# Moving each granule's low product behind the next granule's high products, with a compact delta rule and a later wait for x

## The reference

```python
# gated_delta_rule, chunk length c = 64, 4 chunks, 8 heads (cut)
lower = where(strict, einsum('bhncd,bhnsd->bhncs', kb, k) * decay, 0.0)
tinv = triangular_solve(eye + lower, eye, lower=True, unit_diagonal=True)
u = tinv @ vb
w = tinv @ (kb * exp(g)[..., None])
qk = einsum('bhncd,bhnsd->bhncs', q, k) * decay
def step(state, inp):                      # lax.scan over the 4 chunks
    v_new = un - wn @ state
    o = (qn * exp(gn)[..., None]) @ state + qkn @ v_new
    state = state * exp(g_last) + einsum('bhck,bhcv->bhkv', kn * exp(g_last - gn), v_new)
    return state, o

# hybrid_layer (cut)
x = x + (g_a * (o_a @ w_pa) + g_b * (o_b @ w_pb)) @ w_o
h = rms_norm(x, ln2_w)
return x + square(relu(h @ w_up)) @ w_down
```

## Time and profile before

| what | value |
|---|---|
| median of 3 runs | 2716.54 us (2715.74 to 2717.14) |
| the profiled execution's own time | 2715.65 us |
| its span, first to last instruction | 2714.0 us |
| mean granted clock of TensorE | 0.997 |
| PE busy | 2689.3 us, 99% of the span |
| DVE busy | 1859.4 us, 69% |
| ACT busy | 1288.8 us, 47% |
| POOL busy | 87.3 us, 3% |
| moved by DMA | 504.90 MB, mean 186 GB/s |

### The profile page before, as it was taken

How to read it: one execution, slowest core, us unless ns; L and a number is a source line. 1 busy time by engine, 2 the same in 40 slices (tenths; PEclk the granted TensorE clock), 3 DMA queues, 4 the chain that set the end, 5 groups by cost and what they waited for, 6 DMA issues and landing times.

```text
span 2714.0 us, 35008 instructions
## 1 busy us (share of the span) xinstructions
PE 2689.3 (99%) x12765; PEld 2227.3 (82%) x12765; DVE 1859.4 (69%) x2453; ACT 1288.8 (47%) x1613; POOL 87.3 (3%) x106
## 2 busy tenths in 40 slices
PE   9999999999999999999999999999999999999998
PEld 7888887888888888888888888888888888888886
DVE  5565767765678668586678666775585966668766
ACT  6564646544455444344445555455354434434342
POOL 1000110100000000000000000000000000000000
PEclk9999999999999999999999999999999999999999
DMA  8765555556677666666666566675565656666663
GB/s 243 249 188 142 157 148 145 160 173 188 228 194 198 195 193 193 193 192 195 192 193 192 188 164 183 190 179 200 180 200 166 197 173 190 198 179 190 179 212 122
DMA packets 261739, 504.90 MB, mean 186 GB/s; under 512 B 16456, under 2 KB 25720, under 8 KB 260560
## 3 DMA queue, kind: packets, MB, share of 16 engines
q1 hardware_dynamic: 256848, 486.76, 59.8%
q0 software_dynamic: 4704, 16.03, 2.6%
q10 hardware_dynamic: 32, 0.01, 0.0%
HBM read 498.66 MB, written 4.08 MB: 185 GB/s over the span
## 4 chain that ended last, share of the span: by engine, by line
PE 97%; ACT 1%; DVE 1%; DMA 0%; issue 0%; SPq 0%; DVEq 0%; ACTq 0%
PE acc L296 53%; PE acc L303 27%; PE acc L1965 2%; PE acc L1963 2%; PE acc L1962 2%; PE acc L1923 1%; PE acc L1924 1%; PE acc L1922 1%; PE acc L2080 1%; PE acc L2089 1%; PE mx L511 1%; DMA res<-in_x 0%; PE mx L1741 0%; ACT w_hi L264 0%; PE mx L519 0%; PE mx L343 0%
## 5 line engine op out<-in xcount | busy, mean ns | idle before, releaser
L272 DVE TENSOR_TENSOR w_lo<-raw,w_hi 128x1024 fp32r<-128x1024 f32 x916 | 1121.1, 1226 | 738.0 <-ACT w_hi L264 720.4
L264 ACT ACTIVATE w_hi<-raw 128x1024 fp32r<-128x1024 f32 x916 | 967.7, 1059 | 1234.1 <-PE acc L303 1077.8
L296 PE MATMUL acc<-w_hi,lt_b_hi 128*128 128x512 f32 x1760 | 685.0, 389 | 0.0
L296 PE MATMUL acc<-w_hi,lt_b_lo 128*128 128x512 f32 x1760 | 684.8, 389 | 0.0
L296 PE MATMUL acc<-w_hi,lt_a_hi 128*128 128x512 f32 x1440 | 564.0, 392 | 0.7 <-DVE lt_b_lo L390 0.7
L296 PE MATMUL acc<-w_hi,lt_a_lo 128*128 128x512 f32 x1440 | 562.6, 391 | 0.0
L303 PE MATMUL acc<-w_lo,lt_b_hi 128*128 128x512 f32 x1760 | 476.8, 393 | 0.0
L303 PE MATMUL acc<-w_lo,lt_a_hi 128*128 128x512 f32 x1440 | 394.6, 396 | 1.2 <-DVE w_lo L272 1.2
L296 PEld LDWEIGHTS acc<-w_hi,lt_b_hi 128*128 128x128 f32 x1760 | 330.3, 188 | 68.8
L296 PEld LDWEIGHTS acc<-w_hi,lt_b_lo 128*128 128x128 f32 x1760 | 330.3, 188 | 68.8
L303 PEld LDWEIGHTS acc<-w_lo,lt_b_hi 128*128 128x128 f32 x1760 | 328.7, 188 | 70.3 <-issue 3.8
(11 more groups left out here) (415 smaller groups left out, 1835.1 us busy)
## 6 DMA issues: line engine op xcount, KB each, us to landing
raw<-in_ret_w_in SPq DMA_DIRECT2D x192, 512.0 KB, 4.0
raw<-in_w_in SPq DMA_DIRECT2D x168, 512.0 KB, 3.6
raw<-in_w_up SPq DMA_DIRECT2D x128, 512.0 KB, 3.8
raw<-in_w_down SPq DMA_DIRECT2D x128, 512.0 KB, 4.5
raw<-in_fox_w_in SPq DMA_DIRECT2D x128, 512.0 KB, 4.4
raw<-in_ret_w_out SPq DMA_DIRECT2D x64, 512.0 KB, 4.6
raw<-in_w_o SPq DMA_DIRECT2D x32, 512.0 KB, 4.5
raw<-in_fox_w_out SPq DMA_DIRECT2D x32, 512.0 KB, 4.6
```

The source lines that it names most:

```text
L264: nc.scalar.activation(w_hi[:, r % 4], raw[:, slot, 2 * half:2 * half + 2, :], ACT.Copy).then_inc(hi_ready, 1)
L272: nc.vector.tensor_tensor(w_lo[:, r % 4], raw[:, slot, 2 * half:2 * half + 2, :], w_hi[:, r % 4].bitcast(F32), ALU.subtract) \
L296: nc.tensor.matmul(acc[par][t][:, :], lt[p][:, kt, t * P:(t + 1) * P], w_hi[:, r % 4, k, :], start=(kt == 0 and p == 0), stop=False)
```

## The change

It has three parts.

First, `multiply` is written in another order. The low products become a function `low(r)`. In granule r PE now makes the high products of r, takes the step of the mix, and then makes the low products of granule r-1; the first granule has none, and the job ends with the low products of granule 7. `split_hi`, `split_lo`, `split_job` and their waits stay as they are. In the lines of the new kernel the low products are line 293 and the high ones line 307.

Second, the delta rule's chunk matrices become 64 columns wide: both chunks' blocks stand in the same columns, one above the other on the partitions. `by_chunk` goes; its two operations of 64 x 512 become one of 128 x 512, and ACT's copies of X are half as long. The transposes of Y become 64 x 64 products with the identity, and W, U and the products with `g_qkT` are made of halves. The sums over a chunk are made by one extra product from a small tile `g_sel`, and the masks come in two DMAs.

Third, DVE's wait on `x_again` moves from ahead of the first split of the `J_WO` jobs to just ahead of the add that reads x.

The diff, cut to its core:

```diff
@@ multiply
             wait(pe, acc_taken[par], J.half())
+
+            def low(r):
+
+                wait(pe, lo_ready, J * GPJ + r + 1)
+                for k in range(2):
+                    kt = 2 * r + k
+                    for t in range(NT):
+                        last = nc.tensor.matmul(acc[par][t][:, :], lt[0][:, kt, t * P:(t + 1) * P],
+                                                w_lo[:, r % 4, k, :], start=False, stop=(kt == KT - 1))
+                last.then_inc(granules_done, 1)
+
             for r in range(GPJ):
                 if hook:
                     hook(r)
...
                 step(mix)
-                wait(pe, lo_ready, J * GPJ + r + 1)
-                for k in range(2):
-                    kt = 2 * r + k
-                    for t in range(NT):
-                        last = nc.tensor.matmul(acc[par][t][:, :], lt[0][:, kt, t * P:(t + 1) * P],
-                                                w_lo[:, r % 4, k, :], start=False, stop=(kt == KT - 1))
-                last.then_inc(granules_done, 1)
+                if r:
+                    low(r - 1)
+            low(GPJ - 1)
@@ delta rule, tiles
-        g_X = at(4112, HG, NT, P)
+        g_X = at(4112, HG, NT, CHUNK)
...
+        HALVES = [slice(0, CHUNK), slice(CHUNK, P)]
@@ delta rule, PE
                 def chunk_pair(b, h, t, lhs, rhs):
 
                     i = NT * h + t
-                    for c in range(2):
-                        r = slice(CHUNK * c, CHUNK * c + CHUNK)
-                        o = mx[r, b + i // 4, (i % 4) * P + CHUNK * c:(i % 4) * P + CHUNK * c + CHUNK]
-                        last = MM(o, lhs(r), rhs(r), start=True, stop=True)
+                    for r in HALVES:
+                        last = MM(mx[r, b, i * CHUNK:(i + 1) * CHUNK], lhs(r), rhs(r), start=True, stop=True)
                     return last
...
-                            last = TR(tile(0, h, t), g_Y[:, h, t, :], ident[:, :])
+                            last = chunk_pair(0, h, t, lambda r: g_Y[r, h, t, :], lambda r: ident[r, r])
                     last.then_inc(sg("inv_x"), 1)
...
-                        last = MM(tile(2, h, t), g_kbeg[:, t, h, :], g_Y[:, h, t, :], start=True, stop=True)
+                        i = NT * h + t
+                        for d in HALVES:
+                            for c, r in enumerate(HALVES):
+                                last = MM(mx[d, 2 + c, i * CHUNK:(i + 1) * CHUNK], g_kbeg[r, t, h, d],
+                                          g_Y[r, h, t, :], start=True, stop=True)
                 last.then_inc(sg("uw_ready"), 1)
...
-                        last = MM(tile(0, h, t), g_Y[:, h, t, :], g_vb[:, t, h, :], start=True, stop=True)
+                        i = NT * h + t
+                        for r in HALVES:
+                            last = MM(mx[r, i // 4, (i % 4) * HD:(i % 4 + 1) * HD], g_Y[r, h, t, :],
+                                      g_vb[r, t, h, :], start=True, stop=True)
...
+                pe.wait_ge(sg("taps_ready"), g + 1)
+                MM(mx[:, 3, 0:2 * HG * NT], g_mask[:, M_ONES, 0:1].to_broadcast([P, P]),
+                   g_sel[:, :, :, :].rearrange("p n h t -> p (n h t)"), start=True, stop=True) \
+                    .then_inc(sg("gram_ready"), 1)
@@ delta rule, DVE
                 for l in range(LEVELS):
                     dve.wait_ge(sg("inv_p"), LEVELS * g + l + 1)
-                    by_chunk(g_P1, high_ps, mask(l), ALU.mult).then_inc(sg("inv_p1"), 1)
+                    TT(g_P1[:, :, :, :], p_ps, mask(l), ALU.mult).then_inc(sg("inv_p1"), 1)
                     yield
...
-                    by_chunk(g_Y, g_Y, high_ps, ALU.subtract).then_inc(sg("inv_y"), 1)
+                    TT(g_Y[:, :, :, :], g_Y[:, :, :, :], x_ps, ALU.subtract).then_inc(sg("inv_y"), 1)
@@ the wait for x
-            dve.wait_ge(sg("x_again"), 16)
             split_lo(dve, J_WO, 4, 6)
...
                 if c:
                     norm_block(J_WO + c, B_LN2, LN2, c - 1)
+                else:
+                    dve.wait_ge(sg("x_again"), 16)
                 add_job(J_WO + c, c * NB, "wo_done")
```

More of the change, by code:

```diff
@@ L924, in _ @@
                     for half in range(2):
-                        r = slice(32 * q + BASE * half, 32 * q + BASE * half + BASE)
-                        load(y_tiles[r, :, r], inv_dram[half, q].rearrange("a r c -> r a c"), "inv_loaded")
+                        r, c = (slice(o, o + BASE) for o in (32 * q + BASE * half, 32 * (q % 2) + BASE * half))
+                        load(y_tiles[r, :, c], inv_dram[half, q].rearrange("a r c -> r a c"), "inv_loaded")
                 gdn_root(g, 1, 1)
@@ L1168, in squares, with w_beside_q @@
                         .then_inc(sg("gsq_ready"), 1)
[L1170 to L1174, removed]
+                def w_beside_q():
+                    w_ps = [mx[:, 2 + c, :].rearrange("p (h t s) -> p h t s", t=NT, s=CHUNK) for c in range(2)]
+                    A(g_qw[:, :, CHUNK:2 * CHUNK], w_ps[1][:, :, 0, :], ACT.Copy)
+                    A(g_qw[:, :, 2 * CHUNK:3 * CHUNK], w_ps[0][:, :, 1, :], ACT.Copy)
+                    return A(g_qw[:, :, 5 * CHUNK:6 * CHUNK], w_ps[1][:, :, 1, :], ACT.Copy)
                 columns(0)
@@ L1228, in gdn_mix @@
                 A(g_U[:, :, :, :].rearrange("p (b c) t d -> p b (c t d)", b=2), mx[:, 0:2, :], ACT.Copy)
[L1229 to L1234, removed]
+                A(g_qw[:, :, 0:CHUNK], g_q[:, :, CHUNK:2 * CHUNK], ACT.Copy)
+                A(g_qw[:, :, 3 * CHUNK:5 * CHUNK], g_q[:, :, 2 * CHUNK:4 * CHUNK], ACT.Copy) \
+                    .then_inc(sg("uw_copied"), 1)
                 yield
@@ L1769, in gdn_mix @@
                 if g == 0:
-                    pe.wait_ge(sg("mask_loaded"), 16)
+                    pe.wait_ge(sg("mask_loaded"), 16 * 2)
                     pe.wait_ge(sg("gct_copied"), 4)
                     for t in range(NT):
[L1773 to L1776, removed]
+                        for r in HALVES:
+                            MM(mx[r, 0, t * NH:(t + 1) * NH], g_mask[r, M_TRI, :], tok[r, G_G, t, :],
+                               start=True, stop=True)
+                        for r in HALVES:
+                            last = MM(mx[r, 0, (2 + t) * NH:(3 + t) * NH], g_mask[r, M_ONES, :], tok[r, G_G, t, :],
+                                      start=True, stop=True)
                     last.then_inc(sg("gsum_ready"), 1)
@@ L1781, in gdn_mix @@
                     for t in range(NT):
-                        last = MM(tile(2, h, t), tok[:, G_G, t, hs + h:hs + h + 1].to_broadcast([P, P]),
-                                  g_mask[:, M_TRI, :], start=True, stop=True)
-                last.then_inc(sg("gram_ready"), 1)
+                        chunk_pair(2, h, t, lambda r: tok[r, G_G, t, hs + h:hs + h + 1].to_broadcast([CHUNK, CHUNK]),
+                                   lambda r: g_mask[r, M_TRI, :])
+                pe.wait_ge(sg("taps_ready"), g + 1)
+                MM(mx[:, 3, 0:2 * HG * NT], g_mask[:, M_ONES, 0:1].to_broadcast([P, P]),
+                   g_sel[:, :, :, :].rearrange("p n h t -> p (n h t)"), start=True, stop=True) \
+                    .then_inc(sg("gram_ready"), 1)
                 yield
@@ L1825, in gdn_mix @@
                         for t in range(NT):
-                            last = chunk_pair(2, h, t, lambda r: g_A[r, h, t, r], lambda r: g_Y[r, h, t, r])
+                            last = chunk_pair(2, h, t, lambda r: g_A[r, h, t, :], lambda r: g_Y[r, h, t, :])
                     last.then_inc(sg("inv_p"), 1)
@@ L1838, in gdn_mix @@
                         for t in range(NT):
-                            last = chunk_pair(2, h, t, lambda r: g_X[r, h, t, r], lambda r: g_P1[r, h, t, r])
+                            last = chunk_pair(3, h, t, lambda r: g_X[r, h, t, :], lambda r: g_P1[r, h, t, :])
                     last.then_inc(sg("inv_u"), 1)
@@ L1876, in gdn_mix @@
                         for h in range(HG):
-                            last = MM(mx[:, 3, h * HD:(h + 1) * HD], g_qkT[:, h, t, :], g_V[:, h, :],
-                                      start=True, stop=True)
+                            for c in HALVES:
+                                last = MM(mx[c, 3, h * HD:(h + 1) * HD], g_qkT[c, h, t, :], g_V[c, h, :],
+                                          start=True, stop=True)
                         last.then_inc(sg("in_ready"), 1)
@@ L2408, in gdn_mix @@
                 copy(cwg[:, :, :], cwt[:, :].rearrange("p (c h) -> p c h", h=NH)[:, :, hs])
+                for n, r in enumerate(HALVES):
+                    nc.vector.memset(g_sel[r, 1 - n, :, :], 0.0)
+                    copy(g_sel[r, n, :, :], by_head(tok[r, G_G, :, hs]))
                 nc.vector.memset(g_ct[:, :, 0:3], 0.0).then_inc(sg("taps_ready"), 1)
```

43 lines of the change are left out of this document (20 added, 23 removed).

## The result

The changed kernel takes 2768.82 us (median of 4 runs, 2766.77 to 2772.19) against 2716.4 for the kernel before on the same chip: 1.0191 times as long, interval 1.0179 to 1.0203. That is slower by 52 us; 2760 was forecast, with a range from 2736 to 2784. The profiled execution took 2766.77 us, 51.1 more than that of before.

A forecast was written before the change was run, and what follows sets the result against it. It took PE as the bound, busy 99% of the span, with ACT and DVE marching behind the low products through the ring; its terms added 44.6 us to 2715.65, giving 2760, own range 2740 to 2775, with the clock 2736 to 2784.

The forecast's parts named there:

- The link and its formula: PE-DVE-PE chains in neighbouring steps stall PE by 0.74 us plus d, DVE's operation; 24.2 us over the delta rule.
- The attention's end: PE waits for DVE's last sum, 2.9 us, and the next job for its low part, 2.2 more; 5.1 us.
- ACT's links: PE waits for ACT's answers: three softmax steps 4.3 us, six copies 3.2; 7.5 us together.
- Hooks: Transposes at a granule's head read what DVE made behind an earlier w_lo; three places lose 1.0 each, 3.0 us.
- The wait for x: DVE's wait for the second load of x, moved to the add behind the job, saves PE 1.2 us.
- the loose links, term 5: Nine looser places (steps two apart, silu chains, softmax pieces) lose 0 to 8.2 us; the middle, 4, was taken.
- the clock, term 8: One more dip of PE's granted clock, like that after the silu wait, costs 1.5 us.
- the terms 1 to 5 and 8: Delta rule 24.2 us, attention's end 5.1, ACT's answers 7.5, transposes at granule heads 3.0, looser places 4, clock dip 1.5.
- the compact delta rule, term 7: PE's smaller products in the delta rule add 0.5 us, between -1 and +4; DVE's saving already counted in d.
- The lead only shrinks by one low product: Rival: ACT and DVE answer as soon as PE's step ends, only tight places pay; 2718 us, chance 0.06.
- faster: Rival: the lead harms nobody, the x wait goes and the two silu waits shrink; 2710 us, chance 0.04.
- The clock rival: Repeated stalls halve PE's clock in half of 14 delta-rule granules and one attention turn; 2782 us, chance 0.12.

The follow-up runs named there:

- the step's place: The changed kernel with the step of the mix moved behind the low products of the granule before: 2726.4 us against 2717.57, 1.0028.
- the old order: The changed kernel with the former `multiply`, keeping the compact delta rule and late wait on x: 2712.87 us, 0.998 of the kernel before; repeated, 2712.76 us.
- the ring's release in two parts: The changed kernel, PE's order kept, with w_hi released behind the high products and w_lo behind the low ones: 2726.89 us, 1.003 of the kernel before.
- the order alone: The kernel before with only the new `multiply`, delta rule and wait on x unchanged: 2786.81 us against 2717.57, 1.0246.

## Why the prediction was right, and where its sizes were off

*The link and its formula* (0.74 + d) held. Stalls read as above, from the starts of two PE operations: 11 of about 1.4 us and three of about 1.9 inside jobs (1.43 and 1.86 predicted), 0.5, 0.5 and 1.05 on the first granules (0.52, 0.52, 0.95), nothing on the second ones, 0.9 at the link ahead of the inversion (0.9). The experiments on d, on the step's place and on the release show its three parts one by one.

*The attention's end*: PE waits 2.71 and 2.82 us, shown here in the timeline; 2.9 for each was predicted, 0.7 of the second there before.

```profile
293.12 2.15 DVE L586 SCALAR_TENSOR_TENSOR res<-mx,sm,res 128x128 f32<-128x128 f32 x8
...
295.32 1.09 PE L350 MATMUL mx<-ident,res 128*128 128x128 f32 x8 [2.71 <-DVE res L586]
...
299.75 1.28 DVE L397 TENSOR_TENSOR lt_b_lo<-mx,lt_b_hi 128x512 fp32r<-128x512 f32 x2
...
301.08 0.79 PE L307 MATMUL acc<-w_hi,lt_a_hi 128*128 128x512 f32 x1 [2.82 <-DVE lt_b_lo L397]
```

*ACT's links* came out at the predicted size partly by luck. The list has 4.4 us for the softmax (4.3 predicted), but of its three waits one stood there already:

```profile
PE mx L519 <- ACT arena L538: 1.2, 1, 1.2
```

The earlier trace rows doesn't show this row of the list of before. It belongs to job 6, the compression, which has a loop of its own and not `multiply`'s order, and it is 1.2 us in both kernels. Only the other two softmax steps lost 1.6 each, 3.2 together. One of the copies' steps lost 1.7, and those in fox 1.7 together (3.2 for all six).

*Hooks*: 3.3 by the table, 3.0 predicted. *The wait for x*: 1.5, 1.2 predicted.

*Mis-sized: the loose links, term 5.* It was 4 us. Among them are an answer that needs two engines one behind the other, 2.1 us at L1695 behind DVE, and 3.0 at L1747 behind ACT's L1155, of which the old order has 0.3; silu's waits are 4.5 where the old order has 2.9. With the smaller ones and the products' tails they make some 8 us, by estimate from these waits.

*Mis-sized: the clock, term 8.* It was 1.5 us for one more fall. The granted clock fell behind the attention's end and, for longer, behind the 3.0 us at L1747:

```profile
300.00:308.00 8.00, 6.92 (x32) 5.76 (x33) 2.66 (x9) 4.37 (x9) 1.26 (x2) 0.79 0.52 147
478.00:486.00 8.00, 7.04 (x47) 5.95 (x48) 7.83 (x13) 7.95 (x12) 0.00 (x0) 0.57 0.46 133
```

The share missing from 1.00, times the window's 8 us, gives 1.7 and 3.4 us (an estimate). The fall behind silu before (0.79 from 475 to 483 us, 1.7) is gone, so it's 3.4 us more than before, and 5.1 more than with the old order, which has no such fall.

The order's whole price is 2768.82 - 2712.87 = 56 us by the medians and 54.0 between the profiled spans (2765.1 and 2711.1), where the terms 1 to 5 and 8 made 45.3. Of the 8.7 us between 54.0 and 45.3 the loose links are some 4 and the clock 3.6; about 1 is left for the other terms.

*Mis-sized, with the wrong sign: the compact delta rule, term 7.* I counted PE's small products (+0.5) and DVE's saving only inside the links. With the compact form in and the old order, the jobs 16 to 18 gained 2.6 us, most likely because it also shortened DVE's queue ahead of silu. This miss and the other two partly cancel, which is luck, and why 2760 is as near to 2768.8 as it is. The range had room to spare: its addends make 2745.5 to 2771.5, and it was given as 2740 to 2775.

*The rivals.* "The lead only shrinks by one low product" and "faster" fell: both needed w_lo not to be held by the granule four back, and the ring's release in two parts shows that it was. ACT's waits on the low product are as they were in the earlier trace rows, now 1224.8 us:

```profile
ACT w_hi L264 <- PE acc L293: 1224.8, 631, 6.0
```

The clock rival fell for the changed kernel's links; its other half, a fall at one turn of the attention, took place (the window from 300 us). In the order alone the clock fell in some of the links too. The pairs take 36 ns a record with one bank and with two. The Trainium skill's rule in "TensorEngine Tiling (Array Packing)", section "Restrictions and Gotchas", that different row tiles cannot access the same bank at the same time, changes nothing in these pairs' time; for W's pieces no run tries it. The estimate of 4.6 us took the row's 36 ns for each product, but they are for a record, and a product is two records here (16 products, x32 in the earlier trace rows).

## What to carry to other kernels

Before an engine's work is put off, look for what waits on its end: here hardly anything waited for the low product as a result, but its end released the ring, and two in-order engines answered PE only behind the next refill. A stall in such a chain is the release's lag plus the answer's length minus the time that the asking engine has other work for, and these can be read from one plain granule before anything is run. If one semaphore stands for two buffers that come free at different times, splitting it can be worth more than a new order: here it gave 2.4 us with the old order, and the new order gave nothing.

## What the runs showed of the hardware

Idle times of 1.2 to 1.8 us, one in most granules of the changed kernel's inversion and scan, left PE's granted clock at 1.00. Of those near 2 us in the order alone one was followed by 0.63 over 3.5 us and others by 1.00; the one of 3.0 us in the changed kernel was followed by 0.57 over 8 us. Small products of 64x64 took 36 ns a record in the inversion's pairs, whichever banks they wrote, and 18 ns in W's pieces, where I had expected one price for both.
